# Norms applied behind the product, and the check for crowded experts at expert 1, in a two-block decoder kernel

## The reference, cut to what matters

```python
def rmsnorm(x, g):
    return x * lax.rsqrt(jnp.mean(x * x, axis=-1, keepdims=True) + EPS) * g

# block 1, behind attention
x = x + routed_experts(rmsnorm(x, g_ffn), ...)     # top 4 of 32, weights 1024x2048 and 1024x1024 each
hp = rmsnorm(x, g_ple)
x = x + jax.nn.sigmoid(hp @ w_ple_gate) * (p_i @ w_ple_proj)
# block 2
x = x + 0.5 * swiglu(rmsnorm(x, ffn1_norm))        # silu(h @ w_gate) * (h @ w_up), then @ w_down, 2816 wide
x = x + mixer(rmsnorm(x, mix_norm))
q = rmsnorm(x, mem_q_norm) @ mem_w_q               # keys and values: rmsnorm(mem, mem_kv_norm) @ mem_w_kv
x = x + softmax(q k^T / sqrt(d)) v @ mem_w_o
x = x + 0.5 * swiglu(rmsnorm(x, ffn2_norm))
out = rmsnorm(x, final_norm)
```

## Time and profile before

| | |
|---|---|
| runs | 1946.93, 1947.50, 1948.09 us; median 1947.5 |
| profiled execution | 1947.31 us, its span 1945.5 us |
| busy in the span | PE 86%, DVE 30%, ACT 27%, POOL 22% |
| chain that ended last | PE 57%, DMA 29% (28% of the span is `ring<-in_w_down`), DVE 8%, ACT 4% |
| mean granted clock | 0.965 |

### The profile page before, as it was taken

One profiled execution on the slowest core, in us unless ns is written; L12 is line 12 of the kernel. 1 busy time (PEld: TensorE's weight loads), 2 busy tenths in 40 slices (PEclk: granted clock), 3 DMA queues, 4 the chain that ended last, 5 costly groups with the idle time before them and its releaser, 6 DMA issues.

```text
span 1945.5 us, 21026 instructions
## 1 busy us (share of the span) xinstructions
PE 1678.8 (86%) x9328; PEld 1082.7 (56%) x9329; DVE 586.4 (30%) x714; ACT 531.3 (27%) x706; POOL 421.7 (22%) x124
## 2 busy tenths in 40 slices
PE   7868689888888888888888887899999888889997
PEld 6657543333323323323323224799988767779996
DVE  5684421111111111111111113533332854434322
ACT  5444300000000000000000005544435445444441
POOL 0726600000000000000000004234437333214341
PEclk9989889999999999999999998999999898989999
DMA  6423679999999999999999996555555222425552
GB/s 233 157 87 108 243 288 427 427 428 427 427 428 428 428 428 427 428 427 427 428 428 427 428 427 243 165 165 191 180 188 182 78 87 87 141 87 174 183 185 87
DMA packets 123116, 546.42 MB, mean 281 GB/s; under 512 B 5440, under 2 KB 68032, under 8 KB 98352
## 3 DMA queue, kind: packets, MB, share of 16 engines
q1 hardware_dynamic: 121696, 540.43, 69.9%
q0 software_dynamic: 1040, 4.03, 0.7%
q10 hardware_dynamic: 288, 0.59, 0.1%
HBM read 543.98 MB, written 1.05 MB: 280 GB/s over the span
## 4 chain that ended last, share of the span: by engine, by line
PE 57%; DMA 29%; DVE 8%; ACT 4%; issue 1%; POOL 1%; ACTq 0%; DVEq 0%
DMA ring<-in_w_down 28%; PE PS L683 7%; PE PS L695 7%; PE PS L837 6%; PE PS L487 6%; PE PS L488 6%; PE PS L489 6%; PE PS L473 3%; PE PS L474 2%; PE PS L475 2%; PE PS L648 2%; PE PS L706 2%; PE PS L673 1%; ACT ring L1049 1%; PE PS L459 1%; DVE work L1897 1%
## 5 line engine op out<-in xcount | busy, mean ns | idle before, releaser
L2038 POOL TENSOR_TENSOR ring<-ring,ring 128x2048 fp32r<-128x2048 f32 (+1 forms) x83 | 383.9, 4637 | 765.9 <-ACT ring L1049 765.7
L683 PE MATMUL PS<-ring,work 128*64 128x512 f32 x2048 | 458.3, 596 | 55.6 <-DMA ring<-in_w_gate_up 55.6
L683 PEld LDWEIGHTS PS<-ring,work 128*64 128x64 f32 x2048 | 140.2, 137 | 355.9 <-issue 236.5
L695 PE MATMUL PS<-ring,work 128*64 128x512 f32 x1024 | 236.5, 604 | 71.1 <-DMA ring<-in_w_down 39.1
L1049 ACT CAST ring<-ring 128x2048 fp32r<-128x2048 f32 (+1 forms) x130 | 243.5, 1886 | 70.6 <-DMA ring<-in_ffn_w_down 42.8
L487 PE MATMUL PS<-xr,ring 128*128 128x256 f32 x896 | 255.5, 285 | 1.3 <-DVE xr L1469 1.3
L488 PE MATMUL PS<-xr,ring 128*128 128x256 f32 x896 | 254.5, 284 | 0.0
L489 PE MATMUL PS<-xr,ring 128*128 128x256 f32 x896 | 254.4, 284 | 0.0
L695 PEld LDWEIGHTS PS<-ring,work 128*64 128x64 f32 x1024 | 74.6, 138 | 231.6 <-issue 172.0
L1728 DVE TENSOR_SCALAR work<-PS 128x512 f32<-128x512 f32 x32 | 22.1, 692 | 549.6 <-PE PS L683 549.6
L487 PEld LDWEIGHTS PS<-xr,ring 128*128 128x128 f32 x896 | 173.1, 193 | 1.8 <-ACT xr L1055 0.9
(11 more groups left out here) (353 smaller groups left out, 1767.4 us busy)
## 6 DMA issues: line engine op xcount, KB each, us to landing
ring<-in_w_gate_up SPq DMA_DIRECT2D x128, 2048.0 KB, 20.7
ring<-in_w_down SPq DMA_DIRECT2D x64, 2048.0 KB, 19.4
ring<-in_ffn_w_gu SPq DMA_DIRECT2D x44, 1024.0 KB, 5.1
ring<-in_w_in SPq DMA_DIRECT2D x28, 1024.0 KB, 5.3
ring<-in_ffn_w_down SPq DMA_DIRECT2D x22, 1024.0 KB, 4.8
ring<-in_w_out SPq DMA_DIRECT2D x8, 1024.0 KB, 5.2
ring<-in_mem_w_kv SPq DMA_DIRECT2D x8, 1024.0 KB, 5.2
ring<-in_w_ple_gate SPq DMA_DIRECT2D x4, 1024.0 KB, 7.2
```

Source lines behind the costliest of these rows:

```text
L683: t = e.matmul(PS[hf * 64:hf * 64 + 64, bank, :], XG[g % 2][:, 2 * kp + kk, i * 64:(i + 1) * 64], chunks(raw(w), w)[:, kk, c0 + hf * 512:c ...
L695: t = e.matmul(PS[dh * 64:dh * 64 + 64, BDN, :], HT[:, kk, kp * 64:kp * 64 + 64], chunks(raw(w), w)[:, kk, dh * 512:(dh + 1) * 512], start ...
L2038: e.tensor_tensor(lo(j), raw(j), hi(j).bitcast(F32), ALU.subtract).then_inc(*pool.now(("lo", j)))
```

## The change

1. The side input's weights `w_ple_proj` become one part, loaded ahead of the last `down` instead of two behind it. Its product runs on PE ahead of `down(31)`. `p` is loaded by POOL during the experts instead of before them, and transposed at expert 29. The low halves of `w_ple_proj` and `w_ple_gate` are made by DVE, not POOL.
2. There is one part fewer, so that every later part has the other parity: `mem_k` 0 to 3 go POOL, DVE, POOL, DVE, `ffn1` gate to POOL and up to DVE, `mem_q` 0 to 3 DVE, POOL, DVE, POOL, `ffn2` gate DVE and up POOL.
3. The check for crowded experts moves to the start of expert 1.
4. Four norms (ple, ffn1, memq, ffn2) transpose x itself. The factor is the scale of the sigmoid; in the feed-forward layers it is broadcast by a matmul of ones with a diagonal (`rsb`), multiplied into the gate (on DVE) and into the last residual (`rs_half`); for the memory it goes into the scale of the exponentials. `feats` interleaves the first two weight parts: first half of k of part 0, first half of part 1, second half of part 0, second half of part 1.
5. The final norm goes through its two halves one after another, with one output DMA each.

```diff
+            if e == NE:
+                add("ple_proj", [("w_ple_proj", 0, 2, 0, 1024)])
             if e:
                 add(("down", e - 1), [("w_down", 4 * k, 4, 0, 1024) for k in range(2)], e - 1, False)
-        for b in range(2):
-            add(("ple_proj", b), [("w_ple_proj", 0, 2, b * 512, 512)])
...
-        return i < 6 or (self.parts[i].name[:3] in ("ffn", "mem") and i % 2 == 0)
+        return i < 6 or self.parts[i].name[:5] == "w_ple" or (self.parts[i].name[:3] in ("ffn", "mem") and i % 2 == 0)
...
+            def feats(rT, i0, i1, bank, keys, chunk):
+
+                for kh in range(2):
+                    for z, i in enumerate((i0, i1)):
+                        if kh == 0:
+                            e.wait_ge(*ready(i))
...
             for n in range(NE):
                 g, i = n // 4, n % 4
+                if n == 1:
+                    e.wait_ge(*act["HT", 0])
+                    e.wait_ge(*dve["counts"])
+                    most = e.value_load(cnt[0:1, 32:33], min_val=0, max_val=S)
+                    with e.If(most > CAP):
...
+                    e.wait_ge(*dve["spilled"])
                 gate_up(n)
...
+            (w,) = of["ple_proj"]
+            e.wait_ge(*ready(w))
+            e.wait_ge(*dve["pT", 0])
...
             e.wait_ge(*act["HT", NE - 1])
             down(NE - 1)
             combine(NE - 1)
...
+            def raw_turned(name, dst, t0, norm):
+
+                for i in range(4):
+                    turned(dst, i, t0 + i, norm, (name + "_t", i), name + "T")
+                    if i % 2:
+                        for h in range(2):
+                            squares(name, h, i // 2)
+                for h in range(2):
+                    root(name, h, ss_of[name])
...
             for i in range(4):
                 turned(xT, i, 4 + i, "g_ple", "pleT")
+            lo_to(of["ple_gate", 0][1])
+            raw_root("ple")
...
-                    e.tensor_tensor(o, o, r, ALU.add).then_inc(*dve.now(("x_ple", h, b)))
+                    e.tensor_tensor(o, o, r, ALU.add).then_inc(*dve.now(("x_ffn1", h, b)))
+                lo_to(of["ple_gate", 1][1])
             lo_to(of["mem_k", 0][0])
...
+                if g == 3:
+                    e.wait_ge(*dve["spilled"])
+                    e.dma_start(p_raw, d["p"].rearrange("(h p) n -> p h n", p=128)).then_inc(p_in, 16)
             lo_to(of["ple_gate", 0][0])
-            e.wait_ge(*dve["experts"])
+            e.wait_ge(*dve["x_ple", 1, 1])
             e.dma_start(mem, d["mem_2"].rearrange("(h p) n -> p h n", p=128)).then_inc(mem_in, 16)
...
-            e.wait_ge(*dve["result"])
-            e.dma_start(out.rearrange("(h p) n -> p h n", p=128), x[:, :, :]).then_inc(out_done, 16)
-            e.wait_ge(out_done, 16)
+            for h in range(2):
+                e.wait_ge(*dve["result", h])
+                e.dma_start(out[h * 128:(h + 1) * 128, :], x[:, h, :]).then_inc(out_done, 16)
+            e.wait_ge(out_done, 32)
```

More of the change, by code:

```diff
@@ L1198, in rows_out, with spilled @@
                 e.copy(YRh, PS[:, BDN, :]).then_inc(*act.now(("YR", n)))
+            def spilled(n):
+                e.wait_ge(o_go["act"], 1)
+                e.sem_clear(o_go["act"])
+                for j in range(8):
+                    e.wait_ge(o_v, 2 + 5 * j + 1)
+                    e.activation(osg, ogm, ACT.Sigmoid, scale=1.702).then_inc(o_a, 1)
             for n in range(NE):
@@ L1245, in scalar @@
[L1245 to L1251 removed]
+                if n == NE - 3:
+                    e.wait_ge(*pe["p_t"])
+                    e.copy(pT[0], PS[:, BM, :].rearrange("p (c t) -> p c t", c=2)).then_inc(*act.now(("pT", 0)))
@@ new lines, in scalar @@
+            hi_to(of["ple_proj"][0])
+            for q in range(4):
+                e.wait_ge(*pe["pp", q])
+                e.copy(pp[:, q % 2, (q // 2) * 512:(q // 2) * 512 + 512],
+                       PS[:, BM if q % 2 else BU, :]).then_inc(*act.now(("pp", q)))
+            e.activation(table_out, ident[:, 0:1], ACT.Sqrt).then_inc(*act.now("table1"))
+            rows_out(NE - 1)
+            hi_to(of["ple_gate", 0][1])
+            act.stage("ple")
+            raw_turned("ple", xT, 4, "g_ple")
@@ L1412, in scalar @@
             e.activation(table_out, ident[:, 0:1], ACT.Sqrt).then_inc(*act.now("table3"))
-            for nb in range(2):
-                hi_to(of["out2", 1][0] + 3 + nb)
-                for h in range(2):
-                    squares("mem", h, nb)
+            hi_to(of["mem_q", 0][0])
             act.stage("memory")
-            for h in range(2):
-                root("mem", h, ss_of["mem"])
-            for i in range(4):
-                turned(xT, i, i, "mem_q_norm_2", ("mem_q_t", i), "mem_qT")
+            raw_turned("memq", xT, 0, "mem_q_norm_2")
             for c in range(4):
@@ L1799, in vector @@
+            lo_to(of["ple_proj"][0])
+            rows_rest(NE - 1)
+            for nb in range(2):
+                for h in range(2):
+                    residual("ple", h, nb, BY + 2 * h + nb, ("comb", NE - 1))
             dve.stage("ple")
-            for h in range(2):
-                normalize("after", h, ss_of["after"], x, normed, "n_ple")
             for i in range(4):
                 turned(xT, i, 4 + i, "g_ple", "pleT")
+            lo_to(of["ple_gate", 0][1])
+            raw_root("ple")
@@ L1837, in ffn @@
                     for nb in range(2):
-                        residual(after, h, nb, 4 + 2 * h + nb, (f, "down", h), 0.5)
-            for h in range(2):
-                normalize("ffn1", h, ss_of["ffn1"], x, normed, "n_ffn1", sums="ple")
+                        residual(after, h, nb, d0 + 2 * h + nb, (f, "down", h), rs_half[:, h:h + 1])
             for c in range(4):
@@ L1983, in vector @@
                 for h in range(2):
-                    residual("mem", h, nb, 4 + 2 * nb + h, ("out2", nb, h))
+                    residual("memq", h, nb, 4 + 2 * nb + h, ("out2", nb, h))
+                for i in (2 * nb, 2 * nb + 1):
+                    turned(xT, i, i, "mem_q_norm_2", "memqT")
             dve.stage("memory")
-            for h in range(2):
-                normalize("mem", h, ss_of["mem"], x, normed, "n_mem", sums="mem")
             lo_to(of["mem_q", 0][0] + 1)
-            for i in range(4):
-                turned(xT, i, i, "mem_q_norm_2", "mem_qT")
+            raw_root("memq")
+            e.tensor_scalar(rs_mem, ss_of["memq"], m_scale, None, ALU.mult).then_inc(*dve.now("rs_mem"))
             for c in range(4):
@@ L2123, in spilled @@
                 e.wait_ge(o_v, 2 + 8 * 5 + 4)
+            load_to(of["down", 0][0])
             e.wait_ge(*dve["counts"])
```

379 lines of the change are left out of this document (198 added, 181 removed).

## The result

The changed kernel takes 1974.71 us, the one before 1947.78 in the same session: a ratio of 1.0137, 95% interval 1.012 to 1.0155. It is 27 us slower, where 16 were forecast, and lies above the stated range of 1952 to 1969.

The account below looks back on a forecast made before the run. DMA was taken to bound the experts and PE what follows, with its idle time. Terms 5.7 + 0.6 + 5.7 + 0.5 + 4.2 + 1.0 - 1.8 = +15.9 us gave 1963 us, range 1952 to 1969.

Parts of the forecast that it names:

- The check: At expert 1's start: PE's branch of 4.84 us and a register load delay matmuls and loads, +5.7 us (1.0 to 8).
- p: During the experts: loading 256 KB inside the saturated DMA stretch at 428 GB/s costs +0.6 us.
- the hole isn't made good: At expert 1: the check adds 5.7 us to the DMA hole, and the saturated stretch behind can't win it back.
- From the last expert to mem_k: Stage ple up to mem_k's first result: the late second low half delays it, +5.7 us (about +2 to +9).
- `mem_k` would start without the clock loss: At mem_k's first product: starting behind a short gap, it avoids the earlier loss of 1.9 us.
- The collision: Stage ple: DVE's ple_gate low halves and POOL's mem_k 0 take turns; without this the stage costs about +2 us.
- rsb: In both feed-forward layers: two matmuls of ones and an extra multiply ahead of the first silu, +0.5 us together.
- The query: At the memory's query: PE stands inside feats for POOL's late low half of mem_q 1, +4.2 us (2.7 to 4.9).
- ffn2's start: At ffn2's first products: PE waits behind their first quarter for POOL's low half, +1.0 us (-0.3 to +2.1).
- the end: Final norm: one pass over half of x replaces normalize and L2025, -1.8 us (-1.4 to -2.9 with smaller output DMA).
- The cheap branch: Rival at expert 1: the moved branch costs little, as ACT's 0.05 us suggests, giving 1958 us; chance 0.16.
- The faster rival: Rival at query, ffn2 and ple: second parts split in time, so gaps go, giving 1938 us; chance 0.09.

Follow-up runs that it names:

- e2: Changed kernel with PE's check for crowded experts at expert 8 instead of expert 1: 1964.2 us, ratio to the kernel before 1.0087.
- e3: Changed kernel with the check on all engines back behind the last combine: 1966.2 us, ratio to the kernel before 1.0099.
- e10: e9 with the check at expert 1 again and PE's body of the untaken branch left out: 1936.5 us, ratio to the kernel before 0.9939.
- e9: e7 with mem_k's and ffn1's low halves on the changed kernel's engines (mem_k 0 on POOL): 1939.4 us, ratio to the kernel before 0.9953.
- e5: Changed kernel with ple_gate's low halves back on POOL instead of DVE: 1962.9 us, ratio to the kernel before 1.0081.
- e6: e5 with ple_gate's second column half also cast before the roots on ACT: 1956.9 us, ratio to the kernel before 1.0058.
- e4: Changed kernel with feed-forward and memory low halves on their former engines, and mem_q 1 and ffn2's up 0 cast ahead of the squares: 1955.7 us, ratio 1.0049.
- e11: Changed kernel with p loaded ahead of the experts again: 1970.9 us, ratio to the kernel before 1.0117.
- e1: Changed kernel with the untaken branch's body left out on PE alone: 1963.4 us, ratio to the kernel before 1.0083.
- e7: Changed kernel with the edits of e3, e4 and e6 together: 1943.9 us, ratio to the kernel before 0.9982.

## Why the prediction was wrong

The sign, the places and their order were right. The sizes were too small at two of them, and at both the step that failed is the same: the slow clock behind a wait of PE was put at nothing. One part of the loss was in no term.

**The check** was put at 5.7 and measured 8.4. The branch took 5.85 us and not 4.84 (1.0 more), and the clock it leaves behind was left out: from the first matmul of `gate_up(1)` to the bias matmuls behind it is 17.1 us against 15.6 (281.78 to 298.92, before 271.61 to 287.18), 1.6 more. Idle time 6.9 (7.29 less 0.43) and clock 1.6 make 8.4 or 8.5 of the table's 9.0, and leave 0.5 or 0.6 for p. The step that failed priced the gap without the clock loss, though the same text counted it for the norms' gaps. That the hole isn't made good held (e2 against the changed kernel). That the check cost nothing at its old place in the kernel before was read from its rows and not tested; in the changed kernel it costs 2.8 to 3.5 there (e3, e10 against e9), because the wait that hid it has gone.

**From the last expert to mem_k** was put at 5.7, measured 11.1 at ffn1's product (11.3 and -0.2), and kernels that are alike up to `mem_k` would give 8.8 to 11.1. The order of events was the one forecast: in the time of before (12.2 less) the side product began at 1180.9 (forecast 1181.0), x's transposes began at 1200.4 (1200.1), the first product at 1209.1 (1207.1), the second low half came at 1233.6 (1231.1), `mem_k` began at 1247.7 (1244.0). The steps that failed are those that put the clock at nothing behind a wait. The transposes took 3.55 us instead of 1.91. With that, DVE's last transposed pair was done at 1206.9 and not at 1204.8; the forecast's own terms for this step, 3.8 and 3.2, would have given 1207.1. Behind the second low half, where the sum had taken the mean of a loss and none, 1.2 more were lost up to `mem_k`, with the clock at 0.71 from 1245 to 1249 us. As large as the first is the error of the sentence that `mem_k` would start without the clock loss and so give 1.9 back: the stage was as long as before (28.0 and 28.2). Yet this one was not to be known, since behind the same gap of 2.27 us e5 and e6 kept their clock and took 26.7.

The collision was rightly seen. Its price in the sum was 3.7 us (5.7 with it, about 2 without), and e4 measured 3.9. But it is less than half of what the new order of DVE costs: e5 leaves DVE out and is 9.3 us shorter between the first product and the second low half. The other 5.4 come from low halves that were queued behind instructions that wait for PE. The prediction used that order in its sum, but gave it no price of its own.

**rsb** was put at 0.5 for two layers: ffn1 and the mixer took 382.8 us against 382.5, but the same code took 382.1 to 383.5 in the other kernels, so that the term isn't resolved. **p** at 0.6: 0.5 in e11, not resolved either. **The query** at 4.2: 5.0. The sum was right, the place in part: PE stood 4.38 us ahead of the first product, for DVE's low half, and 1.90 behind its first quarter, for POOL's, where 4 were forecast. e4 shows that engines and casts together take away the second wait and all but 1.51 us of the first. **ffn2's start** at 1.0 and **the end** at -1.8: the end measured -3.0 (7.1 against 10.1), of which 1.3 is the smaller last DMA, which the lower bound had named, and leaves +1.7 for ffn2, where PE stood 6.57 us behind the first quarter and not 4. Right in sum.

**The 3.2 us ahead of expert 1** are in no term. The instructions there are the same but for p's load, and kernels that share them to the letter (changed, e1, e2, e4, e5, e6) reach expert 1's gather between 268.3 and 272.4 us. One place can be seen; windows of the kernel before and of the changed one:

```profile
92.00:96.00 4.00, 4.00 (x38) 3.66 (x35) 1.34 (x2) 2.63 (x2) 3.85 (x2) 1.00 0.01 4
```

```profile
92.00:96.00 4.00, 3.76 (x22) 3.69 (x24) 0.00 (x0) 3.23 (x3) 2.83 (x2) 0.50 0.00 0
```

The same attention matmuls run at 2.4 GHz in one and at 1.2 in the other. Ahead of them PE had stood 1.78 us in the kernel before and 2.15 in the changed one; but in e4 it stood 2.22 us there and kept 2.4 GHz, so that the length of this wait alone doesn't decide it, and what does is open. From this wait to the next long one it is 48.0 us in the changed kernel and 45.3 in the kernel before and in e4: 2.7 of the 3.2. So some 3 of the 27 us of the two profiled executions are not shown to be the change's; a comparison by medians alone is blurred by as much, and the stages are the better measure.

**The rivals.** The cheap branch was wrong (5.85 us). The sentence of the Trainium skill behind it (Advanced Engine Details and Errata, section Control Flow Timing: about 108 ns) doesn't hold for this jump: even e1's short one took twice as long, 0.235 us, and the long one over fifty times. The other page of the Trainium skill (Runtime: NRT & Kernel Launch, section Instruction fetch mechanics) says that a far target waits for a fetch. The trace agrees in so far as the cost goes with the distance, 5.85 us against 0.235; that it is a fetch, no run shows. The faster rival named the right condition: with the second part split in time, query and end come out 3.7 and 8.4 us *below* before (e4), and with all repairs the sign turns, by 0.2% (e7) and 0.5% (e9).

## What to carry to other kernels

A norm factor moved behind the product removes a wait only if the weights are ready at that earlier moment: the casts and low halves have to move with it, and a low half belongs on an engine whose queue has nothing ahead of it that waits for PE. Count for each new gap on PE also the slow matmuls behind it, as a bound, since they come behind some gaps and not behind others of the same length. The branch over a long unrolled body that isn't run cost PE 4.8 to 6.3 us here, so it goes where DMA has free slots to fill or PE waits anyway.
